# A third gate/up weight buffer for the experts of one hybrid decoder step, and another order of the weight requests

## The reference

```python
def expert_block(args):
    xb, e = args
    return (jax.nn.silu(xb @ w_gate[e]) * (xb @ w_up[e])) @ w_down[e]
...
x = x + hier_moe(h2.reshape(Bn * T, D), prm).reshape(Bn, T, D).astype(x.dtype)
...
y_prompt = rmsnorm(xp, norm_final_g)
```

## Time and profile before

| | us |
|---|---|
| median of three runs | 1173.75 |
| lowest and highest of them | 1171.43, 1174.29 |
| profiled execution, its own time | 1169.51 |
| its span in the profile | 1167.7 |

### The profile page before, as it was taken

How to read it: one execution, slowest core, us unless ns; L and a number is a source line. 1 busy time by engine, 2 the same in 40 slices (tenths; PEclk the granted TensorE clock), 3 DMA queues, 4 the chain that set the end, 5 groups by cost and what they waited for, 6 DMA issues and landing times.

```text
span 1167.7 us, 23261 instructions
## 1 busy us (share of the span) xinstructions
PE 1099.2 (94%) x9992; PEld 766.4 (66%) x9992; DVE 494.8 (42%) x985; ACT 357.9 (31%) x814; POOL 303.0 (26%) x197
## 2 busy tenths in 40 slices
PE   5999999999999978888899999899999999999994
PEld 4666666666666667767654544478778887887773
DVE  3200566538865576686644422551112211221134
ACT  3110545554435375765621311110000000000052
POOL 0000000001110169999900000143213332332102
PEclk9999999999999999999999999989999999999998
DMA  6611100001100220002051751268899999999974
GB/s 206 164 36 38 59 19 19 19 19 41 39 24 18 30 44 4 4 4 57 4 203 39 268 211 51 95 250 304 310 342 310 302 336 332 334 303 316 336 292 182
DMA packets 69523, 174.06 MB, mean 149 GB/s; under 512 B 20708, under 2 KB 41895, under 8 KB 65172
## 3 DMA queue, kind: packets, MB, share of 16 engines
q1 hardware_dynamic: 61492, 151.92, 36.7%
q0 software_dynamic: 7920, 20.57, 7.3%
HBM read 147.45 MB, written 27.75 MB: 150 GB/s over the span
## 4 chain that ended last, share of the span: by engine, by line
PE 81%; DVE 11%; DMA 3%; issue 2%; ACT 2%; SPq 1%; POOL 0%; POOLq 0%; DVEq 0%
PE ps L782 23%; PE ps L1499 18%; PE ps L1300 10%; PE ps L1522 8%; DMA arena<-x_dram 2%; PE ps L1528 1%; PE ps L861 1%; PE ps L885 1%; PE ps L874 1%; PE ps L1052 1%; DVE arena L2818 1%; DVE arena L2324 1%; DMA x_dram<-arena,rowB 1%; PE ps L1174 1%; PE ps L1011 1%
## 5 line engine op out<-in xcount | busy, mean ns | idle before, releaser
L782 PE MATMUL ps<-arena 128*128 128x352 f32 (+1 forms) x960 | 296.4, 464 | 2.1 <-issue 1.9
L1499 PEld LDWEIGHTS ps<-arena 128*128 128x128 f32 x2048 | 246.3, 191 | 9.4 <-issue 6.6
L1499 PE MATMUL ps<-arena 128*128 128x128 f32 (+4 forms) x2048 | 248.8, 283 | 2.3 <-DVE arena L2699 1.3
L782 PEld LDWEIGHTS ps<-arena 128*128 128x128 f32 x960 | 179.5, 190 | 105.1 <-issue 9.5
L1522 PE MATMUL ps<-arena 128*128 128x512 f32 x256 | 114.4, 600 | 4.4 <-DVE arena L2699 4.4
L1300 PE MATMUL ps<-arena 128*128 128x512 f32 x256 | 116.4, 597 | 0.7 <-DVE arena L2409 0.7
L2030 ACT ACTIVATE arena<-ps 128x128 f32<-128x128 f32 (+4 forms) x64 | 18.3, 286 | 265.5 <-PE ps L1499 265.5
L2699 DVE TENSOR_TENSOR arena<-arena,ps 128x128 f32<-128x128 f32 (+4 forms) x64 | 19.1, 298 | 185.7 <-ACT arena L2030 185.7
L2894 POOL TENSOR_TENSOR arena<-arena 128x1024 f32<-128x1024 f32 x4 | 11.4, 2860 | 320.4 <-DVE arena L2210 320.4
L1522 PEld LDWEIGHTS ps<-arena 128*128 128x128 f32 x256 | 48.1, 192 | 59.5 <-issue 54.7
L1300 PEld LDWEIGHTS ps<-arena 128*128 128x128 f32 x256 | 46.8, 190 | 52.8 <-issue 51.0
(11 more groups left out here) (426 smaller groups left out, 1514.1 us busy)
## 6 DMA issues: line engine op xcount, KB each, us to landing
arena<-in_w_exp_gate SPq DMA_DIRECT2D x16, 2048.0 KB, 9.6
arena<-in_w_exp_up SPq DMA_DIRECT2D x16, 2048.0 KB, 14.2
arena<-in_w_exp_down SPq DMA_DIRECT2D x16, 2048.0 KB, 12.5
arena<-in_w_in SPq DMA_DIRECT2D x16, 512.0 KB, 3.8
arena<-in_x_prompt SPq DMA_DIRECT2D x9, 512.0 KB, 4.1
x_dram<-arena SPq DMA_DIRECT2D x9, 512.0 KB, 3.6
h_dram<-arena SPq DMA_DIRECT2D x8, 512.0 KB, 2.6
out_y_prompt<-arena SPq DMA_DIRECT2D x8, 512.0 KB, 4.7
```

The source lines that it names most:

```text
L782: last = pe.matmul(ps[:, q % 2, 0:m], wr[:, n % 3, k, :], hT[:, k, a:a + m], start=(k == 0), stop=(k == KB - 1))
L1499: last = pe.matmul(ps[:, 3 + f % 2, n * CAP:n * CAP + CAPS[e]], w[a][:, k, f * P:(f + 1) * P], xgT[:, a, k, 0:CAPS[e]], start=(k == 0), st ...
```

## The change

The region of `X2` becomes a third buffer for gate and up (its first 8 x 1024 columns; the sample rows keep their place behind it). The rows for the final norm go to `XF`, the place of gate/up buffer 1, instead of `X2`. `GU` says which gate/up buffer each place of the order uses: 0, 1, 2 in turn for the first twelve, then 0, 1, 0, 2. Down keeps its two buffers.

SP's loop now runs e from 0 to 13: wait for `gate_up(e)`, then for `down(e)`, request down e+2, and behind it the pair of the next place that uses the buffer which `gate_up(e)` has freed. That is pair e+3 for e = 0 to 10, pair 15 for e = 11 and pair 14 for e = 12. For e = 13 there is none: buffer 1 is free for good, and the residual rows are loaded into it. Pair 2 is requested at the start, behind down 1.

```diff
+        for w, at in ((egate, X20), (eup, X20 + 4096)):
+            w.append(part(at, 4096).rearrange("p (b f) -> p b f", b=KB))
+        XF = ew[:, 12288:12288 + NT * D].rearrange("p (t d) -> p t d", t=NT)
+        final_rows = lambda t: XF[:, t, :] if t < NT else X2[0:NS, NT, :]
+        GU = [0, 1, 2] * 4 + [0, 1, 0, 2]
+        GU_USES = [GU.count(k) for k in range(3)]
...
             x = expert(1)
-            load_pair(x, 1)
+            load_pair(x, GU[1])
             load_part(x, 1, 2)
+            load_pair(expert(2), GU[2])
...
-                for e in range(2, NE):
-                    x = expert(e)
-                    sp.wait_ge(s["gu_ps"], 4 * (NE * r + e - 1))
+                for e in range(NE - 2):
+                    sp.wait_ge(s["gu_ps"], 4 * (NE * r + e + 1))
                     alone(sp)
-                    load_pair(x, e % 2)
-                    if e == NE - 1:
+                    if GU[e] not in GU[e + 1:]:
                         for k in range(2):
                             sp.wait_ge(s[f"yst{k}"], YST[k] * (r + 1))
                             alone(sp)
                         for n, (a, b) in enumerate(XL):
-                            sp.dma_start(X2[:, a:b, :], x_rows[:, a:b]).then_inc(s[f"x{n}"], 16)
-                        sp.dma_start(X2[0:NS, NT, :], x_dram[SEQ:TOK]).then_inc(s["x3"], 16)
-                    sp.wait_ge(s["ya_ps"], NDOWN * r + downs(e - 1))
+                            sp.dma_start(XF[:, a:b, :], x_rows[:, a:b]).then_inc(s[f"x{n}"], 16)
+                        sp.dma_start(final_rows(NT), x_dram[SEQ:TOK]).then_inc(s["x3"], 16)
+                    sp.wait_ge(s["ya_ps"], NDOWN * r + downs(e + 1))
                     alone(sp)
-                    load_part(x, e % 2, 2)
+                    load_part(expert(e + 2), e % 2, 2)
+                    if GU[e] in GU[e + 1:]:
+                        load_pair(expert(e + 1 + GU[e + 1:].index(GU[e])), GU[e])
...
-                pe.wait_ge(s[f"w{a}"], WBASE[a] + 32 * (NE // 2 * r + e // 2 + 1))
+                pe.wait_ge(s[f"w{GU[e]}"], WBASE[GU[e]] + 32 * (GU_USES[GU[e]] * r + GU[0:e].count(GU[e]) + 1))
```

More of the change, by code:

```diff
@@ L690, in one_round @@
                     alone(sp)
[L691 to L694, removed]
-                for e in range(2, NE):
-                    x = expert(e)
-                    sp.wait_ge(s["gu_ps"], 4 * (NE * r + e - 1))
-                    alone(sp)
-                    load_pair(x, e % 2)
-                    if e == NE - 1:
+                    sp.wait_ge(s["fn_dve"], FD * r)
+                    alone(sp)
+                    for e in range(2):
+                        x = expert(e)
+                        load_pair(x, GU[e])
+                        load_part(x, e, 2)
+                    load_pair(expert(2), GU[2])
+                for e in range(NE - 2):
+                    sp.wait_ge(s["gu_ps"], 4 * (NE * r + e + 1))
+                    alone(sp)
+                    if GU[e] not in GU[e + 1:]:
                         for k in range(2):
@@ L713, in one_round @@
                     dst = y_rows[t * P:(t + 1) * P, :] if t < NT else ys_rows
-                    sp.dma_start(dst, X2[0:toks(t), t, :]).then_inc(s[f"h2o{t % 2}"], 16)
+                    sp.dma_start(dst, final_rows(t)).then_inc(s[f"h2o{t % 2}"], 16)
                 sp.wait_ge(s["h2o0"], H2O[0] + 16 * 5 * (r + 1))
@@ L742, in by4 @@
             return ap.rearrange("p (b t) -> p b t", t=DT)
-        WBASE = [w_total(18), w_total(19)]
+        WBASE = [w_total(18), w_total(19), w_total(17)]
         @block.tensor
@@ L1498, in gate_up @@
                     for k in range(KB):
-                        last = pe.matmul(ps[:, 3 + f % 2, n * CAP:n * CAP + CAPS[e]], w[a][:, k, f * P:(f + 1) * P], xgT[:, a, k, 0:CAPS[e]],
+                        last = pe.matmul(ps[:, 3 + f % 2, n * CAP:n * CAP + CAPS[e]], w[GU[e]][:, k, f * P:(f + 1) * P], xgT[:, a, k, 0:CAPS[e]],
                                          start=(k == 0), stop=(k == KB - 1))
@@ L2061, in rows @@
                         act.wait_ge(s["fn_act"], fa + 1 + t)
-                    square(eyA[0:n, 0, :], X2[0:n, t, :], t).then_inc(s["fn_act"], 1)
+                    square(eyA[0:n, 0, :], final_rows(t), t).then_inc(s["fn_act"], 1)
                 def before_last(f):
@@ L2816, in bulk @@
                     n = toks(t)
-                    x = X2[0:n, t, :]
+                    x = final_rows(t)
                     dve.scalar_tensor_tensor(x, x, stat[0:n, 20 + t:21 + t], gfin[0:n, :], ALU.mult, ALU.mult).then_inc(s["fin"], 1)
@@ L2868, in one_round @@
                 dve.wait_ge(s["yo_act"], g0 + NE)
-                dve.tensor_tensor(X2[:, 0, 0:512], xsA[2][:, 0:512], gfin[:, 0:512], ALU.mult)
+                dve.tensor_tensor(XF[:, 0, 0:512], xsA[2][:, 0:512], gfin[:, 0:512], ALU.mult)
                 sums(2, 1)
                 dve.wait_ge(s["yo_dve"], NOUT * (r + 1))
-                again(dve.tensor_tensor(X2[:, 0, 512:], xsA[2][:, 512:], gfin[:, 512:], ALU.mult))
+                again(dve.tensor_tensor(XF[:, 0, 512:], xsA[2][:, 512:], gfin[:, 512:], ALU.mult))
                 dve.wait_ge(s["fn_act"], fa + 16)
                 again(dve.reciprocal(stat[:, 46:47], stat[:, 45:46]))
-                dve.tensor_scalar(X2[:, 0, :], X2[:, 0, :], stat[:, 46:47], None, ALU.mult).then_inc(s["fn_dve"], 1)
+                dve.tensor_scalar(XF[:, 0, :], XF[:, 0, :], stat[:, 46:47], None, ALU.mult).then_inc(s["fn_dve"], 1)
                 assert steps[0] == STEPS
@@ L3028, in _ @@
             pool.wait_ge(s["h2o1"], H2O[1] + 16 * 4 + 16 * 4 * past)
-            for k, out in enumerate((eyA[:, 1, :], eyA[:, 0, :], X2[:, 0, :])):
+            for k, out in enumerate((eyA[:, 1, :], eyA[:, 0, :], XF[:, 0, :])):
                 e = ACC + k
```

## The result

The changed kernel takes 1179.62 us (median of 13 runs, 1177.62 to 1187.43) where the kernel before, measured beside it, took 1174.29. The ratio over all runs is 1.0058, with a 95% interval of 1.0042 to 1.0073: 6.8 us slower (4.9 to 8.6); the two medians alone lie 5.3 us apart. The forecast was 9.9 us slower, with a range that holds the measured time.

What follows compares the result with a forecast made beforehand. TensorE was taken to set the pace in the steady state, with no weight late. Terms +13.3 + 1.8 − 2.87 − 1.8 − 0.5 = +9.9 us on the median 1173.75 gave 1183.7 us, range 1178 to 1188.5.

Steps and rivals of the forecast that it cites:

- rival 1: Loads ahead of gate_up(14, 0) run at their quiet rate, scatter takes nothing: 18.0 us, wait 8.8, time 1179.2; chance 0.09.
- The sum: All priced terms of the change added up: +9.9 us, put on the median of the kernel before.
- wait for pair 14: TensorE stands before gate_up(14, 0) from 1097.2 to 1110.5, three loads taking about 22.5 us: +13.3 us.
- slow clock behind it: Lower granted clock in gate_up(14, 0) and down(13) after the wait for pair 14: +1.8 us.
- squares' wait: ScalarE's squares no longer wait for residual rows, so TensorE's wait ahead of down(14) goes: −2.87 us.
- slow clock behind that: Slow clock in down(14), after the wait ahead of it, goes with that wait: −1.8 us.
- the two other waits: TensorE's waits ahead of gate_up(15, 3) and down(15), 1.29 and 1.52 us, shrink in part: −0.5 us.
- The steady state: Pairs 2 to 13, requested behind a down, still land with 11 us in hand: costs nothing.
- The residual rows: First tile lands at about 1113, all by 1123; ScalarE asks at 1126.5, so its squares wait for nothing.

Runs made afterwards that it cites:

- e3: Changed kernel, but buffers 0 and 1 in turn, requests as before, third buffer loaded once at the start with pair 15; ratio 0.9944 against the kernel before.
- e2: Changed kernel with pair 14 requested ahead of down 14 instead of behind it; ratio 1.0023 against the kernel before.
- e8: Changed kernel without expert 12's scatters and with POOL's gathers held until pair 14 landed; profiled once, no ratio, three loads took 18.7 us.
- e6: Changed kernel without the two scatters of expert 12; ratio 1.0044 against the kernel before.
- e4: Changed kernel with buffers in plain rotation and each pair requested once its buffer is free, ahead of the wait for down; ratio 0.9944 against the kernel before.
- e7: Kernel before, two buffers, with the residual rows requested ahead of pair 15; ratio 1.0032 against the kernel before.
- e9: Second run of e1, the changed kernel with gate/up buffers in plain rotation to the end; ratio 1.0011 against the kernel before.
- e1: Changed kernel with gate/up buffers in plain rotation 0, 1, 2 to the end; ratio 1.0001 against the kernel before.

## Why the prediction was right

The mechanism was the forecast one, at the forecast place: pair 14's late request, a wait ahead of `gate_up(14, 0)`, and no square that waits for rows. The time alone would not show it: 1179.6 is nearer to rival 1 (1179.2) than to the forecast (1183.7). The trace decides: the three loads took 22.1 us and the wait was 12.0, where rival 1 has 18.0 and 8.8. The sum was 2.7 us too high for the stage and 3.1 for the time, so its size is right to about a third. Its terms, as the profile has them, against 9.9 predicted:

| term | predicted us | measured us | from |
|---|---|---|---|
| wait for pair 14 | +13.3 | +12.0 | the row at 1111.41 |
| slow clock behind it | +1.8 | +1.6 | 5.18 for a quarter, where a quarter of the block of 14.45 is 3.6 |
| squares' wait | −2.9 | −2.9 | no wait at 1137.59 |
| slow clock behind that | −1.8 | −1.8 | `down(14)` 7.03 for 8.83 |
| the two other waits | −0.5 | −1.3 | 1.29 gone, 1.52 stayed as 1.53 |
| not priced | 0 | −0.3 | 14.45 for a block of 14.80, 11.21 for 7.31 + 3.84 |
| sum | +9.9 | +7.3 | stage +7.2, timed +6.8 |

**The steady state costs nothing.** Right: TensorE does not wait between 804 and 1097, whatever the new place of the requests. That each pair now comes behind a down, with a register load more, is hidden by the 11 us or so that the pair has in hand. e3 shows the other side of it: two buffers for experts 0 to 14 lose nothing against three.

**Pair 14.** The step was right and the wait 1.3 us too long. About 0.7 of it is the request: SP asked for down 14 at 1089.33, 0.85 us behind the end of `down(12)` (1086.55 + 1.93), where it was 0.52 us before, so the register load behind the wait cost some 0.3 us and not the 1.0 that I read off the start of the stage, where it stands ahead of a first DMA. The rest is the landing, 22.1 us for 22.5. e2 and e8 support its parts: 5.8 us for one load in front (4.9 in the sum), 18.7 for three alone (18.0), 3.4 for what moves beside them (4.4). That the whole came within 0.4 us is in part luck, as the two parts miss by 0.7 and by 1.0 in opposite directions. My way of naming the last part was too narrow: without the scatters the loads are only 1.7 us faster, since a gather takes their place (e6). Two readings behind the sum were loose. The gate that I priced as a load on a quiet queue was requested 2.1 us before down 1 had landed, with gathers under way; it did not matter, as the first load of e8, with nothing beside it, took 7.8 us. And the stretch of 423 GB/s has a gather in it (0.25 of its 2.92 MB), so it is not one of loads alone.

The Trainium skill ("DMA: Bandwidth & Descriptors", Anatomy of one DMA) fits about 2.0 us and the bytes at 436 GB/s to one DMA issued from GpSimd; taken over to three loads in a row on SP's queue that is an estimated 16.4 us. The measured 18.7 us of e8 decide here. The Trainium skill's rule that each DMA engine takes turns between the queue rows (the same page, Queues, rings and completion order) gives no size; that the loads lose 3.4 us to what moves on POOL's queue agrees with it.

**The clock.** Right in size by luck. I carried the 1.8 us behind one wait over to another, and it came out at 1.6; behind the waits for a pair in the other runs a quarter lost 1.8 to 3.0 us (last section). The granted clock was 0.50 for some 2.8 us and full behind that, which is 0.68 over the first 4.5 us, where I had put near 0.6.

**The residual rows.** Right, and shown by e3, e4 and e7: with no pair in front the first tile lands 3.5 to 3.7 us after its request and no square waits; with the rows in front of pair 15, the pair is late instead.

**The two other waits.** This is the term that was mis-sized: I took 0.5 us, for the reason that VectorE's scaling of the rows still stands between its products. It does, but expert 15's first product now comes 3.8 us behind the start of `down(14)`, where it came 6.8 us behind it before, and the whole of the 1.29 us went. The 1.52 us ahead of the last down stayed in every run but e9 (0.69). The trace of the changed kernel shows what stands there:

```profile
1155.66 1.28 DVE L2831 SCALAR_TENSOR_TENSOR arena<-arena,stat 128x1024 f32<-128x1024 f32 x1
...
1156.86 0.28 DVE L2709 TENSOR_TENSOR arena<-arena,ps 128x128 f32<-128x128 f32 x1
...
1155.70 0.28 ACT L2040 ACTIVATE arena<-ps 128x128 f32<-128x128 f32 x1 [0.50 <-PE ps L1509]
```

The silu of the last quarter is done at 1155.98, but VectorE has begun one more row of the final norm and takes the product at 1156.86. So an estimated 0.9 us of this wait is that row; no run tests it.

**What the change could have been.** The third buffer helps the tail only, and there only if both pair 14 and the rows are early. The changed kernel frees the queue for the rows by taking pair 15 first, and pays with pair 14. e4 keeps the plain order and asks for each pair at the moment its buffer is free; e3 fills the third buffer once. Both beat both kernels, by 6.6 us against the one before as timed, by 6.4 (e3) and 5.2 (e4) in the stage.

## What to carry to other kernels

A buffer more bought nothing here where the compute engine did not wait, with the DMA engines at a share of 0.93; look for the few places where it does wait, and read which transfer stands in front of which. On a queue that is worked through in order, a request is to be priced by the time that it is made and by the bytes in front of it, and the last iterations of a loop, where its regular pattern breaks, one by one. Summing a landing time from loads in a row plus what other queues move in that time held within 2% for pair 14, with errors that cancelled; the wait that was expected in e7 for two other transfers on one queue was too low by 4 us, so such a sum wants a margin of some us.

## What the runs showed of the hardware

- With three loads on SP's queue at once, POOL's scatter landed later: the second half took 14.9 us from issue where it took 9.9 before. With three loads it took 14.6 in e1, 15.0 in e2 and 14.3 in e9, and 9.0 in e3, with down 14 alone. That delayed the request of the residual rows from 326.5 to 331.5 us behind the stage's start. In the changed kernel TensorE was late in any case; in e1 the gather of expert 13's rows, which waits for the same scatters, was late with it.
- What a wait costs in clock behind it does not go with its length. Behind waits of 12.02, 10.33, 8.66, 7.25, 6.23 and 2.19 us the quarter of 32 MATMULs took 5.18, 6.60, 5.44, 6.21, 6.56 and 5.47 us, where it takes 3.6 at full clock. Nor is it the same from one execution to the next: the rotation's 3.00 us ahead of `gate_up(15, 3)` was followed by a quarter of 3.84 us in e1, and 3.13 us by one of 5.47 in e9. After the long wait of the changed kernel the clock had fallen to 0.50 while TensorE still stood, and came back some 2.8 us into the quarter (0.50 up to 1114, and 0.97 over the 4 us from there). The Trainium skill ("TensorE: Matmul & The Clock Gate", Part 1) names these two levels; the trace agrees.
